# A hybrid decoder layer on one core: 52 instead of 72 plain fp32 rows in the projections, low parts to row 79 by VectorE, parameters ahead of x, last table doubling on ScalarE

## The chip, the core and the metric

One core of a Trainium2 chip runs the kernel. The metric is the device time of one launch in microseconds (us). Engines are named as the profile names them: PE (TensorE), DVE (VectorE), ACT (ScalarE), POOL (GpSimd), SP (the queue that issues most transfers).

## The reference, cut to what matters

```python
h = x + W_out . concat[ SB(xn), S5(xn), DIFF(xn) ],   xn = RMSNorm(x)
x = h + HMoE(RMSNorm(h));  out = RMSNorm(x)
# SB: stick-breaking attention; S5: complex diagonal state space, GELU + GLU
# DIFF: differential attention; HMoE: top-1 expert group, top-2 experts in it
bu = einsum('blgc,gnc->blgn', u, b_bar);  state_t = lam_bar * state_(t-1) + bu_t
y  = einsum('blgn,gcn->blgc', state, c).real + d_skip * u
```

256 tokens, 2048 channels, all fp32; `w_in` has 2048 x 5120 elements, `w_out` 2048 x 2048, and there are 32 experts.

## The kernel before, in words

**Rows.** The projections are one long run of 224 *rows* on PE. A row is 128 of the 2048 contraction channels times a block of 512 output columns. Ten blocks of 16 rows do `x W_in` (rows 0 to 159, two rows are a *part*, so parts 0 to 79; blocks in order u, sbq, sbk, sbv, dfq, dfk, dfv, dfq, dfk, dfv), and rows 160 to 223 do the output projection with `w_out`. The first `R0` rows are *native*: plain fp32 products (`native_row`, L1608 for the sbv block, L1612 for the others). From row `R0` on, a row is three products of fp32r numbers, high x high, high x low, low x high (`products`, L1586). For these, ACT rounds each weight row to fp32r (`highs`, L633) and POOL subtracts (`lows`, L571) into `w_hi` and `w_lo`, each with four buffers, so that ACT can be three or four rows ahead of PE at most. The low part of x itself (`x_low`, L579) is also POOL's, in place of x, chunk by chunk as the last native rows let go of it.

**What is hung between the rows.** PE's program is written out as `steps[part]`: after a part come the small matmuls of the mixers. `S_STEP` and `Y_STEP` place the eight state pairs of S5 (`s_in` gives the input of a pair to DVE, `s_y` takes its states). `s_pair` on DVE does a pair: products with the phase table `ph`, a scan, products again. Everything later hangs on `Y_STEP[-1]`: `P_GLU` is 3 parts behind it, then SB attention (`P_SB`, `P_SBN`), then four DIFF heads from `P_DF`, and `P_DFN` = `P_DF` + 14, where PE sums squares for the DIFF norm (`df_sums(0)`, L1769). The other four DIFF heads are done between the output rows.

**From the DIFF norm to the output rows.** After `df_sums(0)`, ACT takes roots (`df_roots`, L765) and rounds the mixer outputs in three steps (`y_high(0)`, `(1)`, `(2)`, L772); DVE inverts the roots of two heads (L1174), scales (L1176), makes the low parts of the first two steps (`y_low`, L1201), and inverts and scales the other two heads, which `y_high(2)` waits for. ACT's program in between is

```python
            y_high(0)
            highs(16 * NB - 8)
            y_high(1)
            highs(16 * NB - 4)
            y_high(2)
            evac(9)
```

where `highs(done)` rounds weight rows up to `done + 3`, so that `evac(9)`, which begins with `highs(160)`, is what first rounds rows 160 to 163. The program order of an engine is fixed.

**The start.** x is loaded, squared and transposed; DVE scales the transposed x (L962) and then computes the S5 parameters on 128 x 16 tiles (L923 to L1023), builds `ph` by doubling to 256 steps (L1063 to L1078, the last doubling six instructions of 128 x 2048), and starts the pairs. After the 224 rows come router and experts, whose 192 weight loads of 2 MB each follow the slots that the rows and the experts free.

## Time and profile before

| what | value |
|---|---|
| median of 3 runs | 1412.76 us (1411.92 to 1413.51) |
| the profiled execution: its own time | 1411.37 us |
| its span, first to last instruction | 1409.7 us |
| granted TensorE clock, mean | 0.994 |
| busy: PE, DVE, ACT, POOL | 1351.0, 538.0, 344.8, 228.8 us |
| row 0 starts on PE | 14.06 us |
| first output row (160) starts | 325.31 us |

The profile is of one execution; its time outside the span (1411.37 - 1409.7 = 1.67 us) is launch and end. Times of rows are read from the span's start. A "row" of the profile has `x24` for two or four rows of the kernel: a row of 256-column products has 12 matmuls, one of 512-column products (sbv, dfv, output) has 6, and a plain fp32 matmul stands as two records.

### The profile page before, as it was taken

The numbers are of one execution on the slowest core, as the hardware profiler recorded it, in microseconds if no ns is written. First come the engines' busy times: TensorE is split into PE (matmuls) and PEld (weight loads), VectorE is DVE, ScalarE is ACT, GpSimd is POOL, SyncE is SP. The second block draws the span as 40 slices with busy tenths as digits, with TensorE's granted clock in tenths as the row PEclk, the third lists the DMA queues.
The fourth block names the chain that finished last, engine by engine and source line by source line (L and its number), as shares of the span: only waits on it lengthen the run. The fifth ranks groups of instructions, "written<-read, shape, count | busy, mean of one in ns | idle before, by whom it ended". The sixth has DMA issues, their size and how long they took to land.

```text
span 1409.7 us, 19157 instructions
## 1 busy us (share of the span) xinstructions
PE 1351.0 (96%) x7236; PEld 764.2 (54%) x7236; DVE 538.0 (38%) x1017; ACT 344.8 (24%) x621; POOL 228.8 (16%) x205
## 2 busy tenths in 40 slices
PE   8999999999999999998999999899999999899996
PEld 7884898987786345434433543444543543355442
DVE  6999420444525233223313324222331432324233
ACT  1121378565572111101111111011021111000113
POOL 2002756678782000000000000000000000000000
PEclk9999999999999999999999999999999999999999
DMA  8533643343474999999999999959999999999996
GB/s 215 180 120 119 209 179 120 130 170 134 165 298 192 395 429 426 427 430 427 428 429 428 430 429 427 429 221 429 430 429 428 430 427 430 428 428 428 427 426 262
DMA packets 71540, 471.76 MB, mean 335 GB/s; under 512 B 17329, under 2 KB 17410, under 8 KB 46274
## 3 DMA queue, kind: packets, MB, share of 16 engines
q1 hardware_dynamic: 70834, 469.75, 81.3%
q10 hardware_dynamic: 528, 1.05, 0.2%
q8 instruction: 35, 0.57, 0.2%
q0 software_dynamic: 128, 0.26, 0.1%
q14 instruction: 15, 0.12, 0.0%
HBM read 468.95 MB, written 2.10 MB: 334 GB/s over the span
## 4 chain that ended last, share of the span: by engine, by line
PE 63%; DMA 18%; DVE 2%; ACT 1%; POOL 1%; issue 1%; DVEq 0%; POOLq 0%; ACTq 0%
PE ps L1928 25%; DMA ring<-in_expert_w_dram 18%; PE ps L1946 11%; PE ps L1586 11%; PE ps L1906 5%; PE ps L1936 3%; PE ps L1964 2%; PE ps L1965 1%; POOL w_lo L571 1%; PE ps L1918 1%; PE ps L1853 0%; DVE reg_x L1514 0%; DVE reg_y L1136 0%; PE ps L1878 0%; PE ps L1760 0%
## 5 line engine op out<-in xcount | busy, mean ns | idle before, releaser
L1946 PE MATMUL ps<-ring,reg_y 128*64 128x512 f32 x1056 | 237.3, 602 | 10.7 <-DVE reg_y L1403 8.8
L571 POOL TENSOR_TENSOR w_lo<-ring,w_hi 128x512 fp32r<-128x512 f32 x152 | 199.9, 1346 | 72.5 <-ACT w_hi L633 71.3
L1946 PEld LDWEIGHTS ps<-ring,reg_y 128*64 128x64 f32 x1056 | 75.0, 138 | 146.3 <-issue 142.8
L1409 DVE TENSOR_TENSOR y_lo_t<-ps,y_hi_t 64x512 fp32r<-64x512 f32 x128 | 88.1, 688 | 161.8 <-ACT y_hi_t L867 159.8
L867 ACT ACTIVATE y_hi_t<-ps 64x512 fp32r<-64x512 f32 x132 | 78.1, 592 | 263.6 <-PE ps L1946 262.0
L1417 DVE TENSOR_TENSOR reg_x<-ps,reg_x 128x512 f32<-128x512 f32 x128 | 82.2, 684 | 154.0 <-PE ps L1965 154.0
L1928 PE MATMUL ps<-reg_e,reg_s 128*64 128x512 f32 x528 | 119.4, 594 | 8.9 <-POOLq L596 8.8
L1928 PE MATMUL ps<-ring,reg_s 128*64 128x512 f32 x528 | 120.0, 596 | 7.1 <-POOLq L596 6.6
L1398 DVE TENSOR_SCALAR reg_y<-ps,lamv 128x512 f32<-128x512 f32 x33 | 24.8, 751 | 266.6 <-PE ps L1928 266.6
L1928 PE MATMUL ps<-ring,reg_y 128*64 128x512 f32 x528 | 119.9, 596 | 5.5 <-POOLq L596 5.0
L1928 PE MATMUL ps<-reg_e,reg_y 128*64 128x512 f32 x528 | 119.4, 594 | 2.0 <-POOLq L596 1.6
L633 ACT ACTIVATE w_hi<-ring 128x512 fp32r<-128x512 f32 x152 | 91.6, 630 | 75.8 <-PE ps L1586 65.6
L1612 PE MATMUL ps<-ring 128*128 128x256 f32 x448 | 99.5, 381 | 0.9 <-DMA ring<-in_w_in_dram 0.6
L1612 PEld LDWEIGHTS ps<-ring 128*128 128x128 f32 x448 | 84.1, 190 | 14.4 <-issue 2.6
L852 ACT ACTIVATE reg_y<-ps 128x256 f32<-128x256 f32 x33 | 12.7, 384 | 321.0 <-PE ps L1936 321.0
L1928 PEld LDWEIGHTS ps<-reg_e,reg_s 128*64 128x64 f32 x528 | 37.6, 137 | 85.7 <-issue 69.5
L1928 PEld LDWEIGHTS ps<-ring,reg_s 128*64 128x64 f32 x528 | 35.9, 137 | 81.4 <-issue 64.2
L1928 PEld LDWEIGHTS ps<-reg_e,reg_y 128*64 128x64 f32 x528 | 37.6, 137 | 77.3 <-issue 69.4
L1928 PEld LDWEIGHTS ps<-ring,reg_y 128*64 128x64 f32 x528 | 36.1, 137 | 79.1 <-issue 67.0
L1586 PE MATMUL ps<-w_hi,act_hi 128*128 128x512 f32 x192 | 77.6, 404 | 1.1 <-POOL w_lo L571 1.1
L1586 PE MATMUL ps<-w_hi,act_lo 128*128 128x512 f32 x192 | 75.0, 391 | 0.0
L1586 PE MATMUL ps<-w_lo,act_hi 128*128 128x512 f32 x192 | 74.9, 390 | 0.0
(405 smaller groups left out, 1757.0 us busy)
## 6 DMA issues: line engine op xcount, KB each, us to landing
ring<-in_expert_w_dram SPq DMA_DIRECT2D x128, 2048.0 KB, 20.1
reg_e<-in_expert_w_dram SPq DMA_DIRECT2D x64, 2048.0 KB, 20.4
ring<-in_w_in_dram SPq DMA_DIRECT2D x19, 2048.0 KB, 8.0
ring<-in_w_out_dram SPq DMA_DIRECT2D x8, 2048.0 KB, 7.9
reg_x<-in_x_dram SPq DMA_DIRECT2D x4, 1024.0 KB, 8.5
ring<-in_w_in_dram SPq DMA_DIRECT2D x2, 1024.0 KB, 7.2
out_dram<-reg_x SPq DMA_DIRECT2D x3, 512.0 KB, 2.7
reg_e<-in_ssm_w_glu_dram ACTq DMA_DIRECT2D x1, 1024.0 KB, 9.2
```

What stands on the lines that cost most here:

```text
L571: G.tensor_tensor(w_lo[:, i % BUFS, :], unit(u % SLOTS_A)[:, c, :], w_hi[:, i % BUFS, :], ALU.subtract).then_inc(row_lo, 1)
L633: A.activation(w_hi[:, i % BUFS, :], unit(u % SLOTS_A)[:, c, :], cp).then_inc(row_hi, 1)
L867: A.activation(y_hi_t[64 * q:64 * q + 64, 512 * k:512 * k + 512], psb[3 + k // 2][64 * (k % 2):64 * (k % 2) + 64, :], cp).then_inc(e_yhi, 1)
L1409: V.tensor_tensor(y_lo_t[64 * q:64 * q + 64, w], psb[3 + k // 2][64 * (k % 2):64 * (k % 2) + 64, :], y_hi_t[64 * q:64 * q + 64, w], ALU.su ...
L1417: V.tensor_tensor(xt[:, b, w], psb[6 + k % 2][:, :], xt[:, b, w], ALU.add).then_inc(e_acc, 1)
L1586: last = M(out, lhs[p], rhs[q], start=first and i == 0, stop=last_ and i == 2, skip_group_check=True)
L1612: last = M(banks[ct // 2][:, (ct % 2) * T:(ct % 2) * T + T], w[:, ct * P:(ct + 1) * P], act_x[:, cc, :], start=cc == 0 and ct % 2 == 0, st ...
L1906: last = M(bank[:, o:o + w], part[:, b, c, :], selS[:, b, 0:nq, :].rearrange("p q s -> p (q s)"), start=k == 0, stop=k == 3)
L1928: last = M(psb[m][64 * i:64 * i + 64, :], xeT[half][:, c, 64 * q:64 * q + 64], unit(s)[:, c, :], start=cc < 2, stop=cc >= DC - 2)
L1936: last = M(psb[2][:, 256 * m + 64 * f:256 * m + 64 * f + 64], src[:, f * P:(f + 1) * P], stack2[:, :], start=True, stop=True)
L1946: last = M(psb[3 + i // 2][64 * (i % 2):64 * (i % 2) + 64, :], hT[:, 2 * half + f, :], unit2(s)[:, f, 512 * i:512 * i + 512], start=half = ...
L1964: M(psb[6 + k % 2][:, :], selT[:, b * P:b * P + P], y_hi_t[:, w], start=True, stop=False)
```

## The change

`R0` goes from 72 to 52, and a second mark `R1` = 80 says who makes the low parts: DVE for rows 52 to 79, between the instructions of the state pairs (`low_parts`), with the low parts of x; POOL from row 80. `S_STEP` and `Y_STEP` are new lists, and `Y_STEP[-1]` is 40 where it was 36, so all that hangs on it (`P_GLU` to `P_DFN`) is 4 parts later: `P_DFN` is 77 where it was 73. The S5 parameter transfers are issued ahead of x, the first part of their arithmetic runs before x, the second part between the scalings of x. The last doubling of `ph` is taken apart: ACT makes two products for each of 16 tiles, DVE joins them at the head of each pair (`second_half`). Two bank copies of ACT stand one head earlier (`evac(5)`, `evac(7)`).

```diff
-R0 = 72
+R0 = 52
+R1 = 80
-S_STEP = [9] + [15 + 27 * k // 10 for k in range(ST // 2 - 1)]
-Y_STEP = [17 + (27 * k + 9) // 10 for k in range(ST // 2)]
+S_STEP = [9, 11, 14, 16, 19, 22, 25, 29]
+Y_STEP = [13, 15, 18, 21, 24, 27, 33, 40]
 P_GLU = Y_STEP[-1] + 3
...
-            for b in range(TB):
-                sp.dma_start(xt[:, b, :], x_v[:, b, :]).then_inc(x_in[b], 16)
             sp.dma_start(spar[:, 0, :], lam_re.rearrange("l (j h) n -> (l j) (h n)", h=2)).then_inc(lam_in, 16)
...
+            for b in range(TB):
+                sp.dma_start(xt[:, b, :], x_v[:, b, :]).then_inc(x_in[b], 16)
...
+            def half_products(j):
+                A.activation(ph[:, 0, j, 128:256], ph[:, 1, j, 0:128], cp, scale=sw[:, 3, j:j + 1])
+                return A.activation(ph[:, 1, j, 128:256], ph[:, 0, j, 0:128], cp, scale=sw[:, 3, j:j + 1])
...
+            def second_half(p):
+                v.wait_ge(tab_prod, p + 1)
+                for j in (2 * p, 2 * p + 1):
+                    V.scalar_tensor_tensor(ph[:, 0, j, 128:256], ph[:, 0, j, 0:128], sw[:, 2, j:j + 1], ph[:, 0, j, 128:256],
+                                           ALU.mult, ALU.subtract)
...
+            def x_lows(q):
+                c = X_ORDER[2 * q]
+                v.wait_ge(x_hi, 1)
+                v.wait_ge(row_used, R0 - DC + 2 * q + 2)
+                V.tensor_tensor(act_lo[:, c:c + 2, :], act_x[:, c:c + 2, :], act_hi[:, c:c + 2, :], ALU.subtract).then_inc(x_lo, 2)
+            def v_lows(a_, b_):
+                for i in range(a_, b_):
+                    v.wait_ge(row_hi, i - R0 + 1)
+                    V.tensor_tensor(w_lo[:, i % BUFS, :], unit(i // 8 % SLOTS_A)[:, i % 8, :], w_hi[:, i % BUFS, :],
+                                    ALU.subtract).then_inc(row_lo_v, 1)
+            def low_parts(p, at_):
+                if p == 3 and at_ >= 4:
+                    x_lows(at_ - 4)
...
+                if p >= 6:
+                    i = R0 + 4 + 12 * (p - 6) + 2 * at_
+                    v_lows(i, i + 2)
...
-                pe.wait_ge(row_lo, i - R0 + 1)
+                if i < R1:
+                    pe.wait_ge(row_lo_v, i - R0 + 1)
+                else:
+                    pe.wait_ge(row_lo, i - R1 + 1)
```

The first place is ACT's program from the copy of the last of the first four DIFF heads to the output rows (`w_hi` are `highs`, `act_hi` are `y_high`, L759 or L758 the squares for the norm, L765 or L764 the roots). Before:

```order
L759 ACTIVATE reg_e<-reg_y 128x1024
L649 ACTIVATE reg_d<-ps 128x512 x2
L633 ACTIVATE w_hi<-ring 128x512 x4
L765 ACT_TABLE_LOAD
L765 ACTIVATE reg_e<-ps,lam_s 128x512 x2
L772 ACTIVATE act_hi<-reg_y 128x1024
L633 ACTIVATE w_hi<-ring 128x512 x4
L772 ACTIVATE act_hi<-reg_y 128x1024
L633 ACTIVATE w_hi<-ring 128x512 x4
L772 ACTIVATE act_hi<-reg_y 128x1024
L633 ACTIVATE w_hi<-ring 128x512 x4
```

Now:

```order
L758 ACTIVATE reg_e<-reg_y 128x1024
L639 ACTIVATE reg_d<-ps 128x512 x2
L623 ACTIVATE w_hi<-ring 128x512 x4
L764 ACT_TABLE_LOAD
L764 ACTIVATE reg_e<-ps,lam_s 128x512 x2
L771 ACTIVATE act_hi<-reg_y 128x1024 x3
L623 ACTIVATE w_hi<-ring 128x512 x4
```

The eight weight rows that stood between the three `act_hi` instructions now stand ahead of the table load; the weight rows 160 to 163 stand behind the third `act_hi` as before.

The second place is the head of DVE's last but one pair and what follows in it (L1099 and L1101 are `second_half`, L1143 the pair's first products, L1116 the low parts of weight rows). Before, where a pair has seven kinds of instruction:

```order
L1089 TENSOR_TENSOR reg_d<-ps,reg_e 128x2x2x256 x2
L1094 TENSOR_TENSOR reg_d<-reg_d 128x512
L1095 TENSOR_TENSOR reg_d<-reg_d 128x512
L1099 SCALAR_TENSOR_TENSOR reg_d<-reg_x,reg_d 128x512 x2
L1105 TENSOR_TENSOR reg_d<-reg_d,reg_e 128x1024 x2
```

Now:

```order
L1099 SCALAR_TENSOR_TENSOR reg_e<-reg_e,sw 128x128
L1101 SCALAR_TENSOR_TENSOR reg_e<-reg_e,sw 128x128
L1143 TENSOR_TENSOR reg_d<-ps,reg_e 128x2x2x256
L1116 TENSOR_TENSOR w_lo<-ring,w_hi 128x512 x2
L1143 TENSOR_TENSOR reg_d<-ps,reg_e 128x2x2x256
L1116 TENSOR_TENSOR w_lo<-ring,w_hi 128x512 x2
L1151 TENSOR_TENSOR reg_d<-reg_d 128x512
L1152 TENSOR_TENSOR reg_d<-reg_d 128x512
L1116 TENSOR_TENSOR w_lo<-ring,w_hi 128x512 x2
```

Two low parts stand in each of the six gaps of pairs 6 and 7 (numbered from 0), 24 in all, and four more in pair 5.

The third place is the start of SP's queue (`reg_s` and `dt` are the S5 parameters, `prow` the norm gains). Before, and then now:

```order
L441 DMA reg_x<-in_x_dram 128x2048 x2
L442 DMA reg_s<-in_ssm_lam_re_dram 16x128
L443 DMA reg_s<-in_ssm_lam_im_dram 16x128
L444 DMA dt<-in_ssm_log_dt_dram 16x2
L445 DMA prow<-in_norm_mix_g_dram 16x128
```

```order
L445 DMA reg_s<-in_ssm_lam_re_dram 16x128
L446 DMA reg_s<-in_ssm_lam_im_dram 16x128
L447 DMA dt<-in_ssm_log_dt_dram 16x2
L449 DMA reg_x<-in_x_dram 128x2048 x2
L450 DMA prow<-in_norm_mix_g_dram 16x128
```

Three issues have moved ahead of the two of x; the rest of the queue is as it was.

## Rows read from the trace of the kernel before

**Rows 1.** The page, part 1: busy time and share of the span by engine.
```profile
PE 1351.0 (96%) x7236; PEld 764.2 (54%) x7236; DVE 538.0 (38%) x1017; ACT 344.8 (24%) x621; POOL 228.8 (16%) x205
```

**Rows 2.** Waits of PE, 0 to 450 us: waited, for whom, total, times, longest.
```profile
PE ps L1534 <- DMA reg_x<-in_x_dram: 5.8, 1, 5.8
PE ps L1882 <- DVE reg_s L1291: 2.2, 1, 2.2
...
PE ps L1586 <- POOL w_lo L571: 1.1, 2, 0.6
```

**Rows 3.** Timeline of PE: start us, us, line, operation, tiles, shapes, count.
```profile
108.78 7.13 PE L1608 MATMUL ps<-ring 128*128 128x512 f32 x16
115.84 1.13 PE L1653 MATMUL ps<-reg_y,reg_x 32*128 32x256 f32 x8
...
143.18 10.63 PE L1612 MATMUL ps<-ring 128*128 128x256 f32 x48
...
170.96 7.07 PE L1676 MATMUL ps<-reg_y,reg_e 128*128 128x256 f32 x32
```

**Rows 4.** Chain that ended last, 0 to 420 us: start us, us, what.
```profile
273.99 2.87 PE ps L1586 x24
...
299.22 5.50 PE ps L1586 x24
...
318.27 5.85 PE ps L1586 x24
...
325.31 7.09 PE ps L1586 x30
```

**Rows 5.** Timeline of SP (its queue issues transfers), first five us.
```profile
1.76 0.42 SPq L442 DMA_DIRECT2D reg_s<-in_ssm_lam_re_dram  x1
...
3.31 0.43 SPq L445 DMA_DIRECT2D prow<-in_norm_mix_g_dram  x1
```

**Rows 6.** Timeline of DVE, 34 to 79 us.
```profile
34.22 0.28 DVE L1065 TENSOR_TENSOR reg_d<-reg_e,sw 128x128 f32<-128x128 f32 x1
...
51.48 1.22 DVE L1066 TENSOR_TENSOR reg_d<-reg_e,sw 128x1024 f32<-128x1024 f32 x1
...
55.21 2.29 DVE L1073 TENSOR_TENSOR reg_d<-reg_e,sw 128x2048 f32<-128x2048 f32 x1
...
68.92 2.36 DVE L1089 TENSOR_TENSOR reg_d<-ps,reg_e 128x1024 f32<-128x1024 f32 x2
...
78.01 0.69 DVE L1113 TENSOR_TENSOR reg_x<-reg_d 128x512 f32<-128x512 f32 x1
78.61 2.35 DVE L1089 TENSOR_TENSOR reg_d<-ps,reg_e 128x1024 f32<-128x1024 f32 x2
```

**Rows 7.** Timeline of ACT, 84 us.
```profile
84.70 0.90 ACT L673 ACTIVATE reg_x<-ones,sw 128x255 f32<-128x255 f32 x2 [5.59 <-DVE reg_d L1099]
```

**Rows 8.** Timeline of ACT, 304 to 322 us.
```profile
304.75 0.63 ACT L633 ACTIVATE w_hi<-ring 128x512 fp32r<-128x512 f32 x1 [0.73 <-PE ps L1586]
...
321.36 1.06 ACT L772 ACTIVATE act_hi<-reg_y 128x1024 fp32r<-128x1024 f32 x1 [2.99 <-PE ps L1586]
```

**Rows 9.** Timeline of DVE, 307 to 322 us.
```profile
307.99 3.35 DVE L1174 RECIPROCAL reg_e<-reg_e 128x512 f32<-128x512 f32 x1 [11.70 <-ACT reg_e L765]
...
312.53 4.55 DVE L1201 TENSOR_TENSOR act_lo<-reg_y,act_hi 128x1024 fp32r<-128x1024 f32 x2
317.00 3.34 DVE L1174 RECIPROCAL reg_e<-reg_e 128x512 f32<-128x512 f32 x1
320.38 0.89 DVE L1176 SCALAR_TENSOR_TENSOR reg_y<-reg_y,pcol,reg_e 128x512 f32<-128x512 f32 x1
```

**Rows 10.** Timeline of POOL, 323 us.
```profile
323.01 5.03 POOL L571 TENSOR_TENSOR w_lo<-ring,w_hi 128x512 fp32r<-128x512 f32 x4 [0.60 <-ACT w_hi L633]
```

**Rows 11.** Windows: busy time (instructions) of PE, PEld, DVE, ACT, POOL, then PE's granted clock, DMA share, GB/s.
```profile
441.00:442.00 1.00, 0.00 (x0) 0.00 (x0) 0.88 (x4) 0.00 (x0) 0.00 (x0) 1.00 0.99 426
442.00:447.00 5.00, 4.70 (x12) 2.07 (x13) 4.39 (x26) 0.17 (x1) 0.00 (x0) 0.66 0.31 131
```

More of the change, by code:

```diff
@@ L561, in _ @@
             G.memset(ph[:, 1, :, 0:1], 0.0).then_inc(k_zero, 1)
-            row = [R0]
-            def lows(done):
-                while row[0] < min(done + BUFS, ROWS):
-                    i = row[0]
-                    u, c = i // 8, i % 8
-                    g.wait_ge(row_hi, i - R0 + 1)
-                    G.tensor_tensor(w_lo[:, i % BUFS, :], unit(u % SLOTS_A)[:, c, :], w_hi[:, i % BUFS, :], ALU.subtract).then_inc(row_lo, 1)
-                    row[0] += 1
-                g.wait_ge(row_lo, row[0] - R0)
-            def x_low(chunks):
-                for c in chunks:
-                    g.wait_ge(row_used, R0 - DC + X_ORDER.index(c) + 1)
-                    G.tensor_tensor(act_lo[:, c, :], act_x[:, c, :], act_hi[:, c, :], ALU.subtract).then_inc(x_lo, 1)
-            g.wait_ge(x_hi, 1)
-            x_low(X_ORDER[0:12])
-            lows(R0)
-            x_low(X_ORDER[12:])
-            lows(ROWS)
+            for i in range(R1, ROWS):
+                g.wait_ge(row_hi, i - R0 + 1)
+                G.tensor_tensor(w_lo[:, i % BUFS, :], unit(i // 8 % SLOTS_A)[:, i % 8, :], w_hi[:, i % BUFS, :],
+                                ALU.subtract).then_inc(row_lo, 1)
+            g.wait_ge(row_lo, ROWS - R1)
             g.wait_ge(hp_hi, 4 * TB)
@@ L682, in _ @@
             last.then_inc(x_hi, 1)
-            for p in range(2, 5):
+            for p in range(2, 7):
                 decay(p)
             evac(2)
-            for p in range(5, ST // 2):
-                decay(p)
+            highs(60)
+            decay(7)
             evac(3)
@@ L963, in _, with between @@
                                        ALU.mult, ALU.mult).then_inc(tr_evac_v, 1)
-            v.wait_ge(sp_read, 1)
-            R = lambda i: sw[:, i, :]
-            exp_rows(R(16), R(2), R(5), R(6), R(7), ki[:, :])
-            link(V.tensor_tensor(R(2), R(0), R(16), ALU.mult))
-            link(V.tensor_tensor(R(3), R(1), R(16), ALU.mult))
+            def between(ins, c):
+                n[0] += 1
+                ins.then_inc(vchain, 1)
+                x_evac(c)
+                v.wait_ge(vchain, n[0])
+            for c in range(4):
+                x_evac(c)
             c1 = 6.28125
@@ L972, in _ @@
             c3 = 2 * math.pi - c1 - c2
+            v.wait_ge(sp_angle, 1)
             V.tensor_scalar(R(4), R(2), -87.0, 88.0, ALU.max, ALU.min)
-            link(V.tensor_scalar(R(5), R(3), 1.0 / (2 * math.pi), MAGIC, ALU.mult, ALU.add))
+            between(V.tensor_scalar(R(5), R(3), 1.0 / (2 * math.pi), MAGIC, ALU.mult, ALU.add), 4)
             V.tensor_scalar(R(14), R(4), 1.0 / math.log(2.0), MAGIC, ALU.mult, ALU.add)
-            link(V.tensor_scalar(R(5), R(5), MAGIC, None, ALU.subtract))
+            between(V.tensor_scalar(R(5), R(5), MAGIC, None, ALU.subtract), 5)
@@ L996, in _ @@
-            for k, c in zip((11, 9, 7, 5, 3), (1.0 / 120, 1.0 / 24, 1.0 / 6, 0.5, 1.0)):
-                exp_step(c)
-                V.scalar_tensor_tensor(R(8), R(8), (-1) ** ((k - 1) // 2) / math.factorial(k), R(7), ALU.add, ALU.mult)
-                link(V.scalar_tensor_tensor(R(9), R(9), (-1) ** ((k + 1) // 2) / math.factorial(k + 1), R(7), ALU.add, ALU.mult))
+            between(V.tensor_scalar(R(9), R(7), -1.0 / math.factorial(14), None, ALU.mult), 11)
+            exp_step(1.0 / 120)
@@ L1000, in _ @@
+            between(sine_step(11), 12)
+            exp_step(1.0 / 24)
+            between(sine_step(9), 13)
+            exp_step(1.0 / 6)
+            between(sine_step(7), 14)
+            exp_step(0.5)
+            between(sine_step(5), 15)
+            exp_step(1.0)
+            link(sine_step(3))
             V.scalar_tensor_tensor(R(4), R(14), 1.0, ki[:, :].bitcast(F), ALU.add, ALU.mult)
@@ L1052, in _ @@
             now, nxt = (R(0), R(1)), (R(2), R(3))
-            while w_ < T:
+            while w_ < T // 2:
                 if w_ == 64:
@@ new lines, in _ @@
+                t1, t2, t3, t4 = (reg_d[:, 1024 * i:1024 * i + 1024].rearrange("p (j t) -> p j t", j=ST)[:, :, 0:w_] for i in range(4))
+                V.tensor_tensor(R(5), now[0], now[0], ALU.mult)
+                V.tensor_tensor(R(6), now[1], now[1], ALU.mult)
+                V.scalar_tensor_tensor(nxt[1], now[0], 2.0, now[1], ALU.mult, ALU.mult)
+                V.tensor_tensor(t1, er, pr, ALU.mult)
+                V.tensor_tensor(t2, ei, pi, ALU.mult)
+                V.tensor_tensor(t3, er, pi, ALU.mult)
@@ L1535, in x_transposes @@
                 return last
+            pe.wait_ge(sp_done, 1)
+            for i in range(3):
+                last = TR(at[2][:, 64 + 16 * i:80 + 16 * i], spar[:, i, :], ident[0:16, 0:16])
+            last.then_inc(sT_done, 1)
             pe.wait_ge(x_in[0], 16)
```

111 lines of the change are left out of this document (66 added, 45 removed).

## The prediction

> **What bounds the kernel now.** I read the page first: PE is busy 96% of the span [rows 1], and the chain that ended last runs over PE's projection rows up to about 430 us and then over the experts. Next the waits of PE up to 450 us: the longest are for x at the start and 2.2 us in the router, and PE's rows wait for a low part for 1.1 us in all [rows 2]. So until the last row the time is the sum of what PE has in its program, and a microsecond taken out of a row is one gained, if nothing new has to be waited for. What comes behind the rows hangs on them: the experts' weight transfers start as the last rows give their slots free. I therefore follow the change by one quantity: when does PE start row 160, the first output row, at 325.31 us now [rows 4]? Everything behind it I shift by the same amount.
>
> **What a row costs.** In the sbv block four native rows take 115.84 - 108.78 = 7.06 us, 1.765 each; in the dfq block six take 10.63 us less the 0.07 by which such groups overlap, 1.76 each [rows 3]. In three-product form, two rows of 12 matmuls take 2.87 us, 1.435 each, and four rows of 6 take 5.50 us, 1.375 each [rows 4]. Rows 52 to 63 are the last 12 of sbv, rows 64 to 71 the first 8 of dfq. The change takes out 12 x 0.39 + 8 x 0.325 = **7.3 us**. The number of mixer steps on PE stays the same, only their places move.
>
> **What moves ahead of x.** SP issues the three parameter transfers between 1.76 and 3.31 us [rows 5], so x is issued 1.55 us later. Row 0 waits for the scaled x, which comes by way of x's arrival, the squares, the root and four scalings, so row 0 starts later by the same. Above: 1.55. Below: nothing, if the transfers of x had been waiting for something else than their issue in the first microseconds, which the trace doesn't show. I take **+1.3**, near the issue row. The parameters' 14 linked DVE instructions must then be over when x is there; I count that as covered (the parameter transfers are small and first). Uncovered it would be some tenths, within the bound. The other half of the arithmetic between the x scalings costs PE nothing: DVE needs a scaling ready every 1.76 us.
>
> **The table.** The six 128 x 2048 instructions go from DVE, 68.92 - 55.21 = 13.7 us [rows 6]. In their place each pair begins with four joins of 128 x 128, 0.28 each at most [rows 6], 1.1 a pair. ACT's 32 products are half as wide as the fills of which two take 0.90 [rows 7], so at most 0.45 each, 1.8 a pair against 10.8 of DVE; they lie in ACT's idle time (5.59 in front of that row) and cost nothing. Were that cover gone, DVE's pairs would wait, and through `s_y` PE.
>
> **DVE and PE side by side in rows 52 to 79.** A pair takes 78.61 - 68.92 = 9.69 us now, and one more 128 x 512 subtraction in a queue adds 78.61 - 78.01 = 0.60 [rows 6]. Pairs 6 and 7 then take 9.69 + 1.1 + 12 x 0.60 = 18.0 us each. PE does the 12 rows 56 to 67 in 8 x 1.375 + 4 x 1.435 = 16.7 and one `s_in` of 1.1 [rows 3], 17.8; rows 68 to 79 in 17.2 and one `s_y` of about 1, 18.2. The two are even, and with four buffers neither can lead by more than a few rows. Pairs start earlier: the doubling before the last ends at 55.21 now [rows 6], later by the 1.3 of x and earlier by the parameter steps that went ahead of it, and PE's `s_in(0)`, ten parts of 3.5 behind row 0, comes at the same time, so at about 54 in place of 68.92. Pair 5 then starts at 54 + 5 x 10.8 + 5 x 0.6 for low parts of x = 111 and has the low part of row 52 ready 8 us later, near 119.5. PE, at 115.84 after row 51 now [rows 3], has 1.3 and about four mixer steps of 1.0 to 1.1 more ahead of it: near 121. I take **+0.8** for hand-overs. Below: 0. Above: 4, if a low part costs 0.1 more than 0.60 and the slots come unevenly. Behind each low part PE's row waits, and behind that all of PE; a late DVE also delays ACT's next `highs`.
>
> **What the later steps meet.** `P_GLU` to `P_DFN` are 8 rows later, and PE's own sum doesn't care. But the output rows stay at 160. Now `df_sums(0)` has 12 rows behind it, then only 4. The orders of ACT show it: the first weight row for the output, row 160, is rounded behind the third `act_hi`, and this waits for DVE's second inversion. The chain, from the rounding that PE's row releases:
> - to the start of the first inversion: 307.99 - 304.75 = 3.24 (rounding, table load, roots) [rows 8, 9].
> - inversion, scaling and two `y_low`: 317.00 - 307.99 = 9.01 [rows 9]. Here the two `y_low` took 4.47, while POOL was subtracting. In the new kernel POOL has nothing to do, since ACT rounds nothing: a DVE instruction of the same 128 x 1024 took 1.22 alone [rows 6], and the scaling 0.89 in place of 1.2. So 9.01 - 2.0 - 0.3 = 6.7.
> - second inversion and scaling, to `y_high(2)`: 321.36 - 317.00 = 4.36 [rows 8, 9].
> - `y_high(2)` and the rounding of row 160, to POOL: 323.01 - 321.36 = 1.65, and POOL's 5.03 / 4 = 1.26 [rows 8, 10], with hand-over 1.3.
>
> Together 17.3 us. PE in that time has the sums (two plain 128 x 512 matmuls, as a native row has, 1.8), four rows and `df_scores(4)` (325.31 - 318.27 = 7.04) [rows 4], 8.8, and stands idle for the other 8.5. In the kernel before the same chain ended just in time: `y_high(2)` waited for PE's row [rows 8]. Measured from the rounding at 304.75 (row 147 done), row 160 starts 20.56 us later now [rows 4, 8]; then it is 8 rows, 11.0, and the chain, 17.3, so 28.3: **+7.7**.
>
> The contention that I took out is also the Trainium skill's rule (SBUF — State Buffer, Who interferes with whom): a VectorE instruction with two SBUF inputs and a GpSimd one that reads SBUF block each other. The trace agrees: 2.31 us against 1.22. By the rule the chain is 17.3, without it (the rows as they stand) 19.6.
>
> **The clock.** PE had no work from 441 to 442 us (the router wait of 2.2 us [rows 2]), and over the next 5 us, in which it worked again, its granted clock was 0.66 in the mean [rows 11]: a part at 1.2 GHz, the rest at 2.4 GHz, 5 x 0.34 = 1.7 us of work lost. An idle time of 8.5 us is far longer than that one, so I add the same, **+1.7**. Below: 0, if the clock holds. Above: 3.4, two such stretches.
>
> The Trainium skill says the same of an idle array (TensorE: Matmul & The Clock Gate, What's actually happening): it falls to half rate, and the first work after it runs at half rate.
>
> **The sum.** -7.3 + 1.3 + 0.8 + 7.7 + 1.7 = +4.2 us. The profiled execution took 1411.37 us by its own time, so 1415.6; it lay 1.4 below the median of 1412.76, and against the median the forecast is **1416.9 us**. All lower bounds together (start 0, hand-overs 0, chain 0.3 less, clock 0) give 4.2 - 1.3 - 0.8 - 0.3 - 1.7 = +0.1; all upper ones (1.55, 4, chain 19.6, 3.4) give 4.2 + 0.25 + 3.2 + 2.3 + 1.7 = +11.7.
>
> **Rivals.**
> - *The clock holds.* +2.5 us, 1415.3. For it: PE is idle for 5.8 us at the start [rows 2] and starts without a lower clock on record. Against it: rows 11. Chance 0.14.
> - *DVE falls behind PE in rows 52 to 79.* The even count of 18.0 against 17.8 leaves no reserve. At 4 to 6 us of waits in place of 0.8 the time is 1420 to 1422. Against it: the rows of DVE are regular, and no POOL instruction disturbs them there. Chance 0.16.
> - *Faster: the wait ahead of row 160 is short, and the fp32r rows' gain stays.* Without it the time is 1412.8 - 7.3 + 1.3 + 0.8 = 1407.6. The place is ACT's third `act_hi`. The point from which it decides: with no loss of clock the chain would have to be under 17.3 - 2.5 = 14.8 us to end even, and under 12.0 for faster. The inversions alone are 6.7 of it, and each link is in program order. Chance 0.05.
> - *The start costs nothing and the hand-overs nothing*, with the stall as forecast: +2.1, 1414.9. Chance 0.08.
>
> My forecast has 0.57.
>
> **How the numbers follow.** A measurement of this kernel can tell 0.2%, 2.8 us, from no change. Forecast and the DVE rival end above +2.8 (slower) except for the forecast's lower edge, of which I put 0.04 within. Same: 0.14 + 0.08 less their upper edges 0.04, and 0.04: 0.22. Faster 0.05. Slower 0.73. The range of 8 in 10 leaves out the faster case, the lowest of the same ones, and the uppermost of the DVE rival: 1413.2 to 1421.5.
>
> **What would show it.** Row 0 starts at about 15.4 us in place of 14.06. Rows 52 to 71 are L1647 products, and PE's waits for `w_lo` of DVE up to row 79 are about 1 us together. PE's list of waits gets one new entry of 8 to 9 us near 320 us, at the first output row, put down to POOL's `w_lo` or ACT, with ACT's third `act_hi` released by DVE's scaling in front of it. The granted clock falls to 0.5 around it. Row 160 starts near 328 us. If that entry is absent or under 5 us, the central step is wrong; if row 80 is not reached some 5 us earlier than by the same count now, the row prices or DVE's pace are; if the wait is there but the end moves by less than row 160 did, something behind it has taken it up.

## The result and the profile after the change

The changed kernel takes 1421.55 us (median of 6 runs, 1419.42 to 1422.03), the kernel before 1412.34 us in the same comparison (6 runs, 1411.13 to 1413.51). The ratio is 1.0063, 95% interval 1.0052 to 1.0074: slower, by 9.2 us in the medians. The profiled execution has a span of 1420.0 us against 1409.7, 10.3 us more. The forecast was 1416.9 us, 4.6 us too low, and the measurement lies 0.05 us above the top of the range, 1421.5.

First the page of the changed kernel, part 1. PE is still the engine that is nearly always busy [rows 1], with 2.4 us less work and 10.3 us more span.

```profile
PE 1348.6 (95%) x7292; PEld 770.8 (54%) x7292; DVE 540.7 (38%) x1079; ACT 366.9 (26%) x673; POOL 197.6 (14%) x181
```

So the place to look is the waits of PE, here from 0 to 460 us (waited, for whom, total, times, longest), beside [rows 2].

```profile
PE ps L1647 <- POOL w_lo L573: 8.9, 2, 8.5
PE ps L1600 <- DVE reg_s L938: 3.6, 1, 3.6
PE ps L1647 <- DVE w_lo L1116: 3.5, 3, 1.4
PE ps L1595 <- DMA reg_x<-in_x_dram: 3.0, 1, 3.0
PE ps L1946 <- DVE reg_s L1352: 2.8, 1, 2.8
```

The entry for POOL's `w_lo` was 1.1 us and is 8.9; the one for DVE's `w_lo` is new. The two waits of the start, 3.6 and 3.0, stand for the former 5.8 for x.

How far the changed kernel is from the one before can be read at four places that both programs have. The first is `s_in(0)`, the small PE products ahead of state pair 0. Timeline of PE, the kernel before and then the changed one:

```profile
51.36 1.13 PE L1653 MATMUL ps<-reg_y,reg_x 32*128 32x256 f32 x8
```
```profile
52.68 1.13 PE L1717 MATMUL ps<-reg_y,reg_x 32*128 32x256 f32 x8
...
182.28 7.07 PE L1740 MATMUL ps<-reg_y,reg_e 128*128 128x256 f32 x32
```

The second is the gate product of S5, here 182.28 and before 170.96 [rows 3]; it stands 8 rows later in the new order, and these are rows of 12 matmuls (80 to 87), 1.435 us each. The third is the roots of the first DIFF norm on ACT, 8 rows later as well (148 to 155, of 6 matmuls, 1.375 us each). The fourth is PE's row 160, which has the same number in both. Timeline of ACT, before and then changed:

```profile
306.69 1.27 ACT L765 ACTIVATE reg_e<-ps,lam_s 128x512 f32<-128x512 f32 x2
```
```profile
315.76 0.63 ACT L623 ACTIVATE w_hi<-ring 128x512 fp32r<-128x512 f32 x1 [0.73 <-PE ps L1647]
...
317.70 1.27 ACT L764 ACTIVATE reg_e<-ps,lam_s 128x512 f32<-128x512 f32 x2
...
329.56 1.06 ACT L771 ACTIVATE act_hi<-reg_y 128x1024 fp32r<-128x1024 f32 x1 [8.69 <-DVE reg_y L1237]
```

The chain that ended last, in the changed kernel, from there to row 160 and its neighbours (start, duration, what):

```profile
319.00 3.37 DVE reg_e L1235
...
323.14 2.27 DVE act_lo L1262 x2
325.42 3.27 DVE reg_e L1235
...
330.52 0.62 ACT w_hi L623
...
331.21 1.28 POOL w_lo L573
...
332.57 9.40 PE ps L1647 x30
...
344.20 3.89 PE ps L1647 x17
```

This gives the account of the 10.3 us. At `s_in(0)` the changed kernel is late by 52.68 - 51.36 = 1.3. At the gate product, with 8 rows more behind it (8 x 1.435 = 11.5), it is early by 0.2: 182.28 - 170.96 - 11.5. At the roots, with 8 rows more behind it (8 x 1.375 = 11.0), it is even: 317.70 - 306.69 - 11.0 = 0.0. At row 160 it is late by 332.57 - 325.31 = 7.3 [rows 4]. The five rows from 160 on took 9.40 us instead of 7.09, so row 165 is late by 344.20 - 334.62 = 9.6, and another 0.6 of it is in the router (2.8 us of waiting instead of 2.2).

The windows around row 160 (busy time of PE, PEld, DVE, ACT, POOL, with counts; PE's granted clock, DMA share, GB/s):

```profile
320.00:330.00 10.00, 4.12 (x25) 2.83 (x24) 9.93 (x9) 1.31 (x2) 0.00 (x0) 0.87 0.55 205
330.00:335.00 5.00, 2.43 (x6) 2.00 (x7) 0.69 (x3) 4.97 (x9) 3.79 (x4) 0.50 0.00 0
335.00:340.00 5.00, 5.00 (x19) 3.99 (x18) 1.89 (x6) 3.47 (x11) 3.75 (x4) 0.74 0.00 0
```

PE stops while DVE is 99% busy, mostly with two inversions and the low parts between them; POOL has nothing to subtract, since ACT rounds nothing. When row 160 comes, PE's granted clock is 0.50, the lower of its two levels (1.2 GHz), and it is back only between 335 and 340 us.

### The profile page after: what moved, and what is told of

The parts are those of the page before. It is cut to its first block, busy times and chain, and to the rows that moved or that the text cites. A ratio compares the mean times of both kernels' runs of the same rounds, so it can differ in the third digit from the quotient of the medians.

```text
span 1420.0 us, 19376 instructions
## 1 busy us (share of the span) xinstructions
PE 1348.6 (95%) x7292; PEld 770.8 (54%) x7292; DVE 540.7 (38%) x1079; ACT 366.9 (26%) x673; POOL 197.6 (14%) x181
## 4 chain that ended last, share of the span: by engine, by line
PE 64%; DMA 16%; DVE 3%; ACT 1%; issue 1%; POOL 0%; DVEq 0%; POOLq 0%; ACTq 0%
PE ps L1992 26%; DMA ring<-in_expert_w_dram 16%; PE ps L2010 12%; PE ps L1647 11%; PE ps L1970 5%; PE ps L2000 3%; PE ps L2028 2%; PE ps L2029 2%; PE ps L1982 1%; DVE reg_e L1235 0%; PE ps L1917 0%; PE ps L1942 0%; DVE reg_x L1575 0%; DVE reg_y L1197 0%; PE ps L1824 0%
## 5 line engine op out<-in xcount | busy, mean ns | idle before, releaser
L573 POOL TENSOR_TENSOR w_lo<-ring,w_hi 128x512 fp32r<-128x512 f32 x144 | 185.5, 1316 | 234.0 <-ACT w_hi L623 231.9
L623 ACT ACTIVATE w_hi<-ring 128x512 fp32r<-128x512 f32 x172 | 104.6, 631 | 92.1 <-PE ps L1647 91.9
L1647 PE MATMUL ps<-w_hi,act_hi 128*128 128x512 f32 x216 | 88.2, 408 | 12.5 <-POOL w_lo L573 8.9
L1676 PE MATMUL ps<-ring 128*128 128x256 f32 x384 | 87.0, 383 | 0.0
L1647 PE MATMUL ps<-w_lo,act_hi 128*128 128x512 f32 x216 | 85.2, 394 | 0.0
L1647 PE MATMUL ps<-w_hi,act_lo 128*128 128x512 f32 x216 | 85.2, 394 | 0.0
L1676 PEld LDWEIGHTS ps<-ring 128*128 128x128 f32 x384 | 72.1, 191 | 12.8 <-issue 3.6
```

What stands on the lines that cost most here:

```text
L573: G.tensor_tensor(w_lo[:, i % BUFS, :], unit(i // 8 % SLOTS_A)[:, i % 8, :], w_hi[:, i % BUFS, :], ALU.subtract).then_inc(row_lo, 1)
L623: A.activation(w_hi[:, i % BUFS, :], unit(u % SLOTS_A)[:, c, :], cp).then_inc(row_hi, 1)
L1647: last = M(out, lhs[p], rhs[q], start=first and i == 0, stop=last_ and i == 2, skip_group_check=True)
L1676: last = M(banks[ct // 2][:, (ct % 2) * T:(ct % 2) * T + T], w[:, ct * P:(ct + 1) * P], act_x[:, cc, :], start=cc == 0 and ct % 2 == 0, st ...
```

## The experiments

They were timed in four comparisons, each in rounds with the kernel before, whose median was 1412.9, 1412.9, 1412.4 and 1412.4 us.

**1. The last pair four parts later, alone.** The kernel before, with the one date of `Y_STEP` on which `P_GLU` to `P_DFN` hang (and the two bank copies one head earlier, as the change has them).

```diff
-Y_STEP = [17 + (27 * k + 9) // 10 for k in range(ST // 2)]
+Y_STEP = [17 + (27 * k + 9) // 10 for k in range(ST // 2 - 1)] + [40]
-                if hp == 1:
+                if hp == 0:
                     evac(5)
-                if h == 2:
+                if h == 1:
                     evac(7)
```

> The kernel before with the last of its eight s_y steps at part 40 in place of 36 (so that glu, SB, DIFF and the DIFF norm come 4 parts later) and the two bank copies evac(5) and evac(7) one head earlier, as the change has them; 72 native rows, all low parts by POOL, the table and the start as before. Main theory (the late DIFF norm leaves 4 rows of cover, ACT rounds row 160 behind its third act_hi): this alone costs nearly the whole of the change: a wait of about 8.5 us ahead of row 160, row 160 at about 332.7 us, some 2.3 us of half clock behind it, 1421 to 1423 us. Rival (the low parts on DVE and the start cost the time, the late norm is covered): within 2 us of the kernel before, 1411 to 1414.

Measured: 1423.09 us (1422.28 to 1423.21), ratio 1.0073 [1.0059, 1.0086]. Its chain and its first wait of PE:

```profile
330.78 1.28 POOL w_lo L571
...
332.14 9.70 PE ps L1586 x30
```
```profile
PE ps L1586 <- POOL w_lo L571: 9.0, 2, 8.5
```

With nothing else of the change in it, the kernel shows the same wait, the same slow rows behind it and the whole loss. The later norm of DIFF ahead of a row 160 that has not moved is enough. The two bank copies moved with the date, and no run takes them apart from it; the chain from the roots to row 160 has neither of them in it.

**2. Row 160 rounded ahead of the third `act_hi`.** The changed kernel, in which ACT's order gives rows 160 to 163 their high parts first.

```diff
             y_high(1)
-            highs(16 * NB - 4)
+            highs(16 * NB)
             y_high(2)
```

> The changed kernel with one number: ACT rounds rows 160 to 163 ahead of its third act_hi instead of behind it. Main theory: PE then waits at row 160 only for the first y_low, which ends near 324.2 us, so nearly nothing; row 160 at 324.3 in place of 332.6 and no half clock: 8.3 + 2.3 less, 1411 us. Rival (the wait at row 160 is for something else in the chain, such as POOL, which then stalls further on): less than 4 us gained.

Measured: 1422.48 us (1420.97 to 1423.37), ratio 1.0065 [1.0051, 1.0079]: no gain, and the expectation was missed. Waits of PE, then the timelines of POOL (first row), DVE (second row) and ACT:

```profile
PE ps L1647 <- POOL w_lo L573: 8.0, 2, 7.5
```
```profile
321.22 7.43 POOL L573 TENSOR_TENSOR w_lo<-ring,w_hi 128x512 fp32r<-128x512 f32 x4 [3.10 <-ACT w_hi L623]
...
322.99 4.51 DVE L1262 TENSOR_TENSOR act_lo<-reg_y,act_hi 128x1024 fp32r<-128x1024 f32 x2
...
331.64 1.06 ACT L771 ACTIVATE act_hi<-reg_y 128x1024 fp32r<-128x1024 f32 x1 [8.29 <-DVE reg_y L1237]
...
336.58 1.67 ACT L623 ACTIVATE w_hi<-ring 128x512 fp32r<-128x512 f32 x3
```

The four rows ran early and the wait stood behind them, at row 164. So the stall does not hang on the place of row 160's rounding, but on everything that ACT has from the third `act_hi` on: that instruction waits 8.29 us for DVE, then come the bank copy, a table load and the exponentials of head 4, and the next rounding is at 336.58. The early rows also gave POOL work, from 321.22 to 328.65 us, and DVE's two `y_low` beside it took 4.51 us instead of 2.35. That is the rule of the Trainium skill (SBUF — State Buffer, Who interferes with whom) by which a VectorE instruction with two SBUF inputs and a GpSimd one that reads SBUF block each other; the trace agrees.

**3. The new order around row 160.** The changed kernel; ACT leaves the third `act_hi` until head 5, and DVE the norm in front of it until after the maximum of head 5.

```diff
             y_high(1)
-            highs(16 * NB - 4)
-            y_high(2)
             evac(9)
...
                 highs(rows_out(0) + DF_ROWS[h - 3])
+                if h == 5:
+                    y_high(2)
                 df_copy(h)
...
             y_low(1)
-            df_norm(2, 2).then_inc(ny, 1)
             for h in range(4, DFH):
                 df_max(h)
                 if h == 5:
+                    df_norm(2, 2).then_inc(ny, 1)
+                if h == 6:
                     y_low(2)
```

> The changed kernel with the third y_high and y_low, and the norm of state blocks 4 and 5 of DIFF ahead of them, put behind the next heads: VectorE does the norm after the maximum of head 5 and y_low(2) at head 6, ScalarE does evac(9), the high parts and exponentials of heads 4 and 5 first and y_high(2) at head 5. Main theory (row 160 waits because its high part is rounded on ScalarE behind a third act_hi that waits for a norm which the move of the last eight plain rows has made late): the wait of TensorE for w_lo from GpSimd at row 160 (9.0 us in two waits, 8.5 the longest) falls below 1.5 us, row 160 begins near 324 to 326 us instead of 332.57, the half clock after it goes too, and the time falls by 7 to 10 us to 1411.5 to 1414.5 us. A new wait can arise where y_high(2) stands now: up to 3 us at rows 168 to 176, 1415 to 1417 us. Rival (the rest of the stage, and not this wait, sets the date of the rows behind it, for instance VectorE's own chain through the scores): the wait moves to another line and the time stays at 1420 to 1422 us.

Measured: 1415.55 us (1413.60 to 1416.05), ratio 1.0018 [1.0009, 1.0027]: 6.0 us less than the changed kernel, 1.0 short of the expected 7 to 10. The waits of PE that are left near row 160, and the chain:

```profile
PE ps L1648 <- DVE act_lo L1262: 1.5, 1, 1.5
...
PE ps L1648 <- POOL w_lo L573: 0.5, 1, 0.5
```
```profile
325.08 8.70 PE ps L1648 x30
...
346.49 6.86 PE ps L1648 x30
```

Row 160 is at 325.08 as expected. But the output stage still costs more than in the kernel before. There the third group of rows began at 343.68 and the roots at 306.69; here the same rows are at 346.49 and the roots at 317.12. Less the 11.0 of the eight rows the stage costs 3.4 us more than before; in the changed kernel it costs 9.6. Of the 3.4, 0.3 lies ahead of row 160, 1.6 in the five rows from it on (8.70 us instead of 7.09), and 1.4 ahead of the third group, where PE waits for DVE behind the moved norm. The expectation that the half clock goes too was missed: PE waited only 1.55 us ahead of row 160, and yet its granted clock was at the lower level behind it.

```profile
326.00:328.00 2.00, 2.00 (x7) 1.54 (x6) 2.00 (x5) 0.00 (x0) 2.00 (x2) 0.50 0.00 0
```

**4. PE kept at work through the stall.** The changed kernel, with nine matmuls behind `df_scores(4)` whose results nothing reads, about as long as the stall.

```diff
             df_scores(4)
+            for _i in range(9):
+                M(at[2][:, :], ident[:, :], reg_d[:, 2048:2560], start=True, stop=True)
```

> The changed kernel with nine plain fp32 128x512 matmuls into an unused bank behind df_scores(4), where PE waits for row 160; their results are not used. Main theory: the clock falls in that wait and the first output rows take 9.4 us in place of 7.1; with the idle time filled, the clock stays at full speed, row 160 still starts at about 332.6, time 2.3 us less, 1419.2. Rival (the slow first rows come from POOL and ACT, not from the clock): first five output rows still 9 us, time the same.

Measured: 1419.03 us (1418.04 to 1419.75), ratio 1.0043 [1.0029, 1.0057]: 2.5 us less than the changed kernel. Windows of this kernel:

```profile
320.00:330.00 10.00, 10.00 (x38) 5.28 (x37) 9.81 (x11) 1.31 (x3) 0.00 (x0) 1.00 0.49 187
330.00:340.00 10.00, 8.97 (x40) 6.33 (x40) 2.06 (x7) 8.47 (x20) 8.54 (x7) 1.00 0.00 0
```

The clock stayed at its upper level, and no row was slow. Row 160 came as long after the roots as in the changed kernel (14.9 us), and the five rows and the small steps to row 165 took 341.69 - 331.77 = 9.9 us instead of 344.20 - 332.57 = 11.6. That is 1.7 us and not the whole 2.3, because rows 160 to 163, now faster, met a wait of some tenths for POOL at row 164. So the stall has two prices: its own 7.3 us, and 2.3 us of slow rows behind it, of which 1.7 can be had back here. The Trainium skill's sentence on the idle array (TensorE: Matmul & The Clock Gate, What's actually happening) says that it falls to half rate after idling, and the trace agrees on both sides: with work it shows 1.00, without it 0.50.

**5. The third decay ahead of a bank copy.** In the changed kernel, pair 2 starts at 75.69 us, and its scan waits. Timelines of DVE and ACT in the changed kernel:

```profile
84.22 2.34 DVE L1157 TENSOR_TENSOR_SCAN reg_d<-reg_x,reg_d 128x512 f32<-128x512 f32 x2 [3.69 <-ACT reg_x L663]
```
```profile
78.47 1.08 ACT L636 ACTIVATE reg_s<-ps 128x512 f32<-128x512 f32 x2 [17.36 <-PE ps L1676]
79.44 3.89 ACT L680 ACTIVATE act_hi<-ring 128x1024 fp32r<-128x1024 f32 x4
83.23 1.69 ACT L663 ACTIVATE reg_x<-ones,sw 128x255 f32<-128x255 f32 x4
```

ACT's fill with decay factors for pair 2 (L663) stands in its order behind `evac(1)`, which waits for the end of PE's row 31 and had left ACT idle for 17.36 us, and behind the four high parts of x. The edit:

```diff
+            decay(2)
             evac(1)
...
-            for p in range(2, 7):
+            for p in range(3, 7):
                 decay(p)
```

> The changed kernel with ACT's fill of the decay tile for state pair 2 ahead of the bank copy evac(1), not behind it. In the changed kernel DVE's scan of pair 2 waits 3.7 us for it, and PE later waits 3.5 us for DVE's low parts. If the second comes from the first: DVE's wait gone, PE's waits for w_lo of DVE under 1 us, time 2.5 to 3 us less, 1418.8. Rival (DVE's pace in pairs 5 to 7 makes PE wait, as 18.0 against 17.8 us allows): PE's waits stay above 2.5 us and the time within 1 us.

Measured: 1417.76 us (1416.42 to 1418.43), ratio 1.0037 [1.0023, 1.0051]: 3.8 us less. Timelines of DVE and PE of this kernel:

```profile
79.75 2.34 DVE L1158 TENSOR_TENSOR_SCAN reg_d<-reg_x,reg_d 128x512 f32<-128x512 f32 x2
```
```profile
51.87 1.13 PE L1718 MATMUL ps<-reg_y,reg_x 32*128 32x256 f32 x8
...
178.16 7.07 PE L1741 MATMUL ps<-reg_y,reg_e 128*128 128x256 f32 x32
```

From `s_in(0)` to the gate product PE took 126.29 us, 3.3 less than the changed kernel's 129.60, and of its waits for DVE's `w_lo` (3.5 us) this was left:

```profile
PE ps L1648 <- DVE w_lo L1117: 0.6, 1, 0.6
```

DVE's pair 5 started at 110.47 us, where the forecast had 111, and not at 114.94 as in the changed kernel: DVE kept the pace that had been worked out, once its decay factors came in time. The 8.5 us stall was still there, at the same length, 4.1 us earlier: the two losses add.

**6. The start: parameters on another queue.** The changed kernel, with the three parameter transfers issued on ACT's queue, so that SP issues x first.

```diff
-            sp.dma_start(spar[:, 0, :], ...).then_inc(lam_in, 16)
-            sp.dma_start(spar[:, 1, :], ...).then_inc(lam_in, 16)
-            sp.dma_start(dt2[:, :], ...).then_inc(lam_in, 16)
+            a.dma_start(spar[:, 0, :], ...).then_inc(lam_in, 16)
+            a.dma_start(spar[:, 1, :], ...).then_inc(lam_in, 16)
+            a.dma_start(dt2[:, :], ...).then_inc(lam_in, 16)
```

> The changed kernel with the three parameter transfers issued on ScalarE's queue at the start of its program, so that x is again the first thing that SyncE issues. In the changed kernel SyncE issued x at 2.22 us instead of 0.85, x[1] reached VectorE at 9.85 us instead of 8.33 and row 0 began at 15.88 instead of 14.06. If the place on SyncE's queue is what costs the start, row 0 goes back to about 14.4 us and the total falls by about the same 1.4 us, to 1420.2 us; VectorE's pairs still have their dates from their own chain, so the waits for w_lo (3.5 us in the changed kernel) may grow a little by as much as rows come sooner, which would eat 0.3 to 1 us of it. If instead the parameter steps of VectorE ahead of x are what delays row 0, row 0 stays at 15.5 us or later and the total stays at 1421.5 us. If ScalarE's own early work (the split of x) is delayed by its three issues, row 0 stays too.

Measured: 1423.76 us (1422.57 to 1425.13), ratio 1.0079 [1.0065, 1.0093], 2.2 us more than the changed kernel. Neither time came true: it got slower. DVE's parameter steps ahead of x are the reason, as in the second way, but the parameters came later than in the changed kernel. Transfers of this kernel (count, size, median us to landing) and DVE's timeline:

```profile
reg_s<-in_ssm_lam_re_dram ACTq DMA_DIRECT2D x1, 8.0 KB, 3.0
reg_s<-in_ssm_lam_im_dram ACTq DMA_DIRECT2D x1, 8.0 KB, 5.4
dt<-in_ssm_log_dt_dram ACTq DMA_DIRECT2D x1, 0.1 KB, 5.6
```
```profile
7.36 0.21 DVE L938 COPY reg_s<-dt 16x128 f32<-16x128 f32 x1 [6.39 <-DMA dt<-in_ssm_log_dt_dram]
...
11.90 1.22 DVE L949 SCALAR_TENSOR_TENSOR reg_y<-reg_x 128x1024 f32<-128x1024 f32 x1
```

In the changed kernel the three landed 1.6, 1.6 and 1.5 us after their issue. Issued beside x, of which SP had issued 2 MB from 0.85 us on, 0.1 KB took 5.6 us. In the kernel before, behind x on SP's own queue, the three took 6.7, 6.4 and 6.1 us: here it counts what else is under way, and not the queue. DVE's first parameter step was at 7.36 us instead of 3.26, and its part of x, behind those steps, at 11.90 instead of 9.85. The Trainium skill has a rule for it (DMA: Bandwidth & Descriptors, Issuing engines are not separate DMA queues): transfers from any engine interleave on the same 16 DMA engines, and another queue only saves the time of the issue. The trace agrees that they interleave, with 1.5 against 5.6 us.

**7. The start: parameters first, alone.** The kernel before, with the three transfers ahead of x on SP's queue and nothing else changed.

```diff
+            sp.dma_start(spar[:, 0, :], ...).then_inc(lam_in, 16)
+            sp.dma_start(spar[:, 1, :], ...).then_inc(lam_in, 16)
+            sp.dma_start(dt2[:, :], ...).then_inc(lam_in, 16)
             for b in range(TB):
                 sp.dma_start(xt[:, b, :], x_v[:, b, :]).then_inc(x_in[b], 16)
```

> The kernel before with one part of the change alone: SyncE issues the three parameter transfers ahead of x; VectorE's program is that of before. If the three issues (1.37 us in the changed kernel's rows) are the cost of the start, x[1] reaches VectorE 1.4 us later than before's 8.33 us, row 0 comes 1.4 us after 14.06, and the time rises by 1.4 us, to about 1413.8 us. If VectorE's part of the prologue has slack that takes it up later (before waited 0.6 us for a transfer into the ring near 44 us and 1.1 us for VectorE's pairs), 0.5 to 1 us are left of it, 1413 us. If the delay of x costs nothing, 1412.4 us.

Measured: 1414.06 us (1412.69 to 1414.93), 1.7 us over the 1412.37 us of before; ratio 1.0009 [1.0000, 1.0018], about what can be told from nothing. x[1] reached DVE at 9.71 us instead of 8.33, later by 1.38, as expected. In the profiled execution more was lost: `s_in(0)` came 3.1 us later, and the reason is in PE's timeline of this kernel.

```profile
12.44 1.19 PE L1549 MATMUL ps<-reg_y,ones 128*128 128x256 f32 x2 [0.66 <-DVE reg_y L950]
...
13.99 3.25 PE L1534 MATMUL ps<-ident,reg_x 128*128 128x128 f32 x14
```

Before, the same two groups took 0.67 and 1.75 us. Here PE ran them at half its pace, though the records show a granted clock of 1.00 there. The last section comes back to it.

**8. The edits together.** Three kernels from the changed one, each with the edits of experiments 3 and 5: as it is (parameters first on SP's queue), with `lam_im` alone on ACT's queue, and with `lam_im` and `log_dt` on ACT's queue. A fourth has all three on ACT's queue. The fifth is the second with ACT's idle time of 3.17 us at 321 us filled:

```diff
-                highs(rows_out(0) + DF_ROWS[h - 4])
+                highs(rows_out(0) + DF_ROWS[h - 4] + (2 if h == 4 else 0))
```

The two edits, parameters first on SP's queue:

> The changed kernel with the third decay ahead of evac(1) and the new order around row 160, and the start left as in the changed kernel (parameters first on SyncE's queue). Alone the two edits gave 3.8 and 6.0 us. If they are separate terms: 1421.5 - 3.8 - 6.0 = 1411.7 us (1410.5 to 1413), and against the kernel with parameters on ScalarE's queue as well (1415.2 us) 2.2 to 3.5 us faster, which would show that the place on SyncE ahead of x is the cheaper one. If row 160 and its neighbours only wait longer when the rows before come sooner, 1413.5 to 1415.5 us, with 2 us or more of new waits between 320 and 350 us.

One transfer on ACT's queue:

> The kernel of the two edits with one of the three parameter transfers (the imaginary parts) on ScalarE's queue, and the real parts and log_dt first on SyncE's, so that x is issued at 1.76 us instead of 2.22 and no parameter is issued after x. If the issues ahead of x are the cost of the start, row 0 comes 0.46 us earlier and the time falls by 0.5 us, to about 1411.2 us, against the kernel with all three on SyncE; nothing of it if VectorE's parameter steps end later than x lands.

Two on ACT's queue:

> The kernel of the two edits with two of the three parameter transfers (the imaginary parts and log_dt, in this order) on ScalarE's queue, so that x is issued at 1.30 us and log_dt on the other queue at the same moment. With all three on ScalarE's queue the last parameter landed at 7.36 us instead of 3.26 and VectorE's steps, which stand ahead of its part of x, began that much later. If a small transfer waits for what x has put ahead of it, log_dt lands at 5 to 7.4 us here too, row 0 comes at 16.5 to 17.5 us and the time is 1 to 3 us over that of the kernel with all three on SyncE. If being issued no later than x is enough, it lands by 3.5 us, row 0 comes 0.9 us earlier and the time falls by about 1 us.

All three on ACT's queue:

> The changed kernel with three edits together: the third decay ahead of evac(1) on ScalarE (measured alone: 3.8 us faster), the parameter transfers on ScalarE's queue, and the new order around row 160. If the three causes are separate terms that add: 1421.5 - 3.8 - 1.4 - 8.5 = 1407.8 us, range 1405.5 to 1411, faster than the kernel before by 0.1 to 0.5%. If each frees time that the next wait takes back (row 160 comes sooner by 5 us where the norm comes no sooner), 1411 to 1415 us with a wait of 3 us or more at POOL's w_lo or at VectorE's tables.

Rows 164 and 165 rounded earlier:

> The kernel of the two edits and the divided parameter transfers, in which ScalarE rounds the high parts of two more rows (164 and 165) ahead of the exponentials of head 4, where it sat idle for 3.17 us (321.4 to 324.56 us). There TensorE waited 1.3 us at 328.20 and 0.5 us before for w_lo from GpSimd. If those waits are what ScalarE's order costs, they go and the time falls by 1.3 to 1.8 us, to 1409.4 to 1410 us, which would be 0.2% under the kernel before. If the end of the row after is set by VectorE (a wait of 1.5 us for the low part of y stays at row 160, and DIFF's norms behind head 4 come later by what ScalarE's exponentials are later), nothing is gained: 1411.2 us, with the wait under VectorE's name.

The fourth row of the table is from an earlier comparison than the others.

| kernel | median us (11 runs each) | ratio to before |
|---|---|---|
| two edits | 1411.71 (1410.58 to 1412.72) | 0.9992 [0.9983, 1.0001] |
| one transfer on ACT's queue | 1411.23 (1409.41 to 1413.16) | 0.9989 [0.9980, 0.9998] |
| two on ACT's queue | 1411.69 (1410.78 to 1412.11) | 0.9995 [0.9986, 1.0004] |
| three on ACT's queue | 1415.23 (1413.57 to 1418.29) | 1.0019 [1.0010, 1.0028] |
| one on ACT's queue, rows 164 and 165 earlier | 1411.78 (1410.70 to 1412.71) | 0.9997 [0.9988, 1.0006] |

The two edits add as expected: 1421.55 - 3.8 - 6.0 = 1411.75, measured 1411.71. Ahead of row 160 PE waits 1.55 us here too, but its granted clock stays at 1.00, and it waits 1.3 us for POOL at row 164 in place of the slow rows; from the roots to the third group it takes 343.53 - 314.20 = 29.3 us, as in experiment 3 (29.4). By this comparison the slow rows of experiment 3 hardly cost anything: ACT and DVE set the time of that stretch. All three on ACT's queue cost 3.5 us more, the same sign as in experiment 6 (2.2 us). Dividing the transfers is worth 0.5 us by the medians where x is issued 0.44 us earlier (1.78 instead of 2.22), which the spread of the runs does not resolve; with `log_dt` issued beside x it landed 3.0 us after its issue instead of 1.5, and nothing was left of the gain. The best, 1411.23 us, is 10.3 us under the changed kernel and 0.1% under the kernel before: its interval leaves out 1, but the gain is smaller than the 0.2% that I set as the bound.

The last one was a miss, and its rival was right. The waits of PE at POOL's `w_lo` fell to 0.5 us (1.8 in the kernel it was made from), and a new one for DVE took their place. PE's timeline of the fifth kernel, and its chain:

```profile
330.92 0.55 PE L1816 MATMUL ps<-ident,reg_e 128*128 128x128 f32 x3 [1.71 <-DVE reg_e L1251]
```
```profile
343.46 6.85 PE ps L1649 x30
```

From the roots to the third group of output rows it took 343.46 - 314.16 = 29.3 us, and the second kernel 342.56 - 313.22 = 29.3. ACT's exponentials of head 4, behind the two roundings, delayed DVE by what POOL had gained.

## Why the prediction came out as it did

The sign, the mechanism and the place were right: the wait stood at row 160 with 8.5 us where 8.5 had been worked out (in part by luck: the chain was 0.5 us shorter than its sum, and PE's own work in it 0.4 shorter), POOL's `w_lo` was named, the third `act_hi` was released by DVE's scaling after 8.69 us. The total was 4.6 us too low, and nearly all of it is in two terms that lie ahead of the roots, each 2.5 us too favourable. Step by step:

- **The rows, -7.3.** Too much. In the kernel of experiment 5, where PE hardly waits, the stretch from `s_in(0)` to the gate product takes 126.29 us, with 8 rows of 1.435 us more in it than before: 126.29 - 11.5 = 114.8, against 170.96 - 51.36 = 119.6. That is -4.8. The prediction held that only the places of the mixer steps move. But a step also breaks the run of rows, and in the kernel before an `s_y` and an `s_in` often stood together in one break. Timeline of PE, twelve unbroken rows before and two between breaks in the kernel of experiment 5:

```profile
52.43 20.99 PE L1612 MATMUL ps<-ring 128*128 128x256 f32 x96
```
```profile
69.19 3.72 PE L1677 MATMUL ps<-ring 128*128 128x256 f32 x16
```

Less the overlap of 0.07 that is 1.74 us a row against 1.825, so some 0.2 us for each break. Rows 20 to 51, native in both kernels, stood in 5 groups and now stand in 11: from `s_in(0)` to the `s_in` behind row 51 PE took 115.84 - 51.36 = 64.5 us before and 120.57 - 51.87 = 68.7 there, of which three more steps are 3.0, so 1.2 us were lost before the first row of three products. Another 0.6 is the wait that was left; the remaining 0.7 lies behind row 51, and no run separates it.

- **The start, +1.3.** Measured +1.3 at `s_in(0)`, and 1.38 from the issue alone in experiment 7. The first figure hits so well by luck: `s_in(0)` came at 51.36 and 50.46 us in the two profiled executions with the start of before (51.36 has a wait of 0.58 us for a weight transfer in it), and between 51.87 and 52.68 in the six that start as the changed kernel does.
- **Hand-overs of DVE and PE, +0.8.** Measured 3.3, by experiment 5, and by another mechanism than the one I had bounded. I had taken ACT's part of the pairs as lying in idle time. Its work did, but its order didn't let it: pairs that start 15 us earlier need their decay factors earlier, and the third stands behind a wait for PE's row 31. This is the step that failed, beside the rows. The rival "DVE falls behind PE" had the right place, 3.5 us of waits for DVE's `w_lo`, and its 1420 to 1422 us hold the measured time; but the cause is ACT and not the load of DVE, since those waits fell to 0.6 us when only ACT's order was changed.
- Together to the roots of the norm: -5.2 forecast, 0.0 measured. So all that the fp32r rows gain is used up before the expensive part begins.
- **The wait ahead of row 160, +7.7.** Measured +7.3 (late by 0.0 at the roots, by 7.3 at row 160). The chain was 332.57 - 315.76 = 16.8 us against 17.3. Experiment 1 shows that the four parts in the date (with the two bank copies) are its cause, and experiment 3 that most of it goes when the third norm step and its `act_hi` are moved behind row 160.
- **The clock, +1.7.** Measured +2.3 in the rows, and 2.6 and 1.8 in the kernels of experiments 1 and 5 behind the same wait of 8.5 us; taken away by itself in experiment 4 for 2.5 us in the medians and 1.7 in the trace. The rival "the clock holds" is out.
- Behind it the forecast said that all shifts by the same. It did, but for 0.6 us in the router.

Row 0 came at 15.88 us and not at 15.4: the half pace on PE that experiment 7 met. In the kernels of experiments 4 and 5, which start alike and did not meet it, it came at 15.41. Row 160 came at 332.57 and not near 328, which is the missing 5.2 less the 0.4 by which the wait's term was too high. The sum itself has a slip of rounding: 1412.76 + 4.2 is 1417.0 and not 1416.9.

## What to carry to other kernels

When a date in a static order moves, list for every engine what stands between the instruction that needs its input sooner and the one ahead of it: an engine that is idle for three quarters of the time can still deliver late, because it waits in its order for somebody else's row. When small steps are moved between long runs of rows, count the breaks and not only the steps. When the work ahead of a fixed deadline is moved later, count the cover left (here 12 rows to 4) against the whole chain of small instructions behind it, and look whether a piece of that chain is needed at all before the deadline. A transfer that must come first has to be issued first; another queue does not bring it ahead of a large one.
